# First FFN begun on x*(1+scale) with the shift as a bias vector, and the depthwise convolution as 16 channels by 8 phases

## The reference, cut

```python
mod = (silu(c) @ w_ada + b_ada)              # 9 D: sh1 sc1 gt1 sh2 sc2 gt2 sh3 sc3 gt3, scale as 1 + sc
h = x * (1 + sc1) + sh1
gt, up = split(h @ ffn1_w_in)                # hidden width 2816
x = layer_norm(ALPHA * x + 0.5 * gt1 * ((silu(gt) * up) @ ffn1_w_out))
h = x * (1 + sc2) + sh2
a, b, u, gate_a, gate_b = split(h @ w_in)    # 1024 columns each
glu  = a * sigmoid(b)
conv = causal_depthwise_conv(glu, width 31) + conv_b
y_a  = silu(layer_norm(conv)) @ w_conv_out
pooled = trailing_mean(u, window 2, 4, 8 or 16 by channel group) - u
y_b  = (group_matmul(pooled, pool_w) * pool_scale) @ w_pool_out
x = layer_norm(ALPHA * x + gt2 * ((sigmoid(gate_a) * y_a + sigmoid(gate_b) * y_b) @ w_out))
# then a second half-step FFN like the first, with sh3 sc3 gt3
```

## Time and profile before

| | |
|---|---|
| median of 3 runs | 1577.0 us (1576.28 to 1577.05) |
| the profiled execution | 1571.3 us; span on its slowest core 1569.7 us |
| spans of the 8 cores | 1556.7 to 1569.7 us, granted TensorE clock 0.992 to 0.995 |
| busy on the slowest core | PE 1479.4, PEld 856.3, DVE 688.6, ACT 472.9, POOL 133.9 us |
| DMA engines | mean 145 GB/s moved; the weight queue's packets took 48.6%, SP's 20.9% of 16 engines' span |
| chain that ended last | PE 84%, DMA 9%, DVE 3%, ACT 2%, issue 2% |

### The profile page before, as it was taken

How to read it: one execution, slowest core, us unless ns; L and a number is a source line. 1 busy time by engine, 2 the same in 40 slices (tenths; PEclk the granted TensorE clock), 3 DMA queues, 4 the chain that set the end, 5 groups by cost and what they waited for, 6 DMA issues and landing times.

```text
span 1569.7 us, 24460 instructions; the slowest of 8 cores (1556.7 to 1569.7 us)
## 1 busy us (share of the span) xinstructions
PE 1479.4 (94%) x9258; PEld 856.3 (55%) x9258; DVE 688.6 (44%) x935; ACT 472.9 (30%) x688; POOL 133.9 (9%) x253
## 2 busy tenths in 40 slices
PE   0799999999899999999999999999999999999995
PEld 0466666544344457765664564445666665444454
DVE  1223323565222465972377687237431134441255
ACT  0011112253112264672127456113531111421124
POOL 2011111000110000000000000000000010000000
PEclk9999999999999999999999999999999999999998
DMA  9989999869977868635386964457586465584522
GB/s 185 180 141 196 196 215 186 167 110 190 186 137 145 144 155 232 182 72 131 55 174 143 243 182 105 97 104 154 118 178 131 74 132 97 111 170 84 113 70 99
DMA packets 94980, 227.03 MB, mean 145 GB/s; under 512 B 10848, under 2 KB 36192, under 8 KB 94688
## 3 DMA queue, kind: packets, MB, share of 16 engines
q0 software_dynamic: 37136, 124.11, 48.6%
q1 hardware_dynamic: 57728, 101.36, 20.9%
HBM read 299.64 MB, written 40.11 MB: 216 GB/s over the span
## 4 chain that ended last, share of the span: by engine, by line
PE 84%; DMA 9%; DVE 3%; ACT 2%; issue 2%; SPq 0%; DVEq 0%; ACTq 0%; POOL 0%; POOLq 0%
PE ps L354 78%; PE ps L769 4%; DMA VS<-pool_w 3%; DMA ring<-ffn_w_in 2%; DMA VS<-R 2%; DMA XS<-tp_dr 1%; DMA ring<-w_ada 1%; DVE VB L322 1%; PE ps L418 1%; DVE hA L319 1%; ACT L315 1%; ACT scr L315 0%; PE ps L544 0%; ACT rstd_sb L315 0%; ACT VB L315 0%
## 5 line engine op out<-in xcount | busy, mean ns | idle before, releaser
L354 PE MATMUL ps<-hA,ring 128*128 128x348 bf16 x3072 | 467.2, 312 | 8.1 <-DMA ring<-ffn_w_in 3.6
L354 PE MATMUL ps<-hB,ring 128*128 128x512 bf16 x2048 | 450.9, 380 | 10.0 <-DVE mpv L513 5.3
L354 PE MATMUL ps<-R,ring 128*128 128x348 bf16 (+3 forms) x2378 | 398.7, 327 | 0.0
L354 PEld LDWEIGHTS ps<-hA,ring 128*128 128x128 bf16 x3072 | 298.1, 97 | 170.1 <-issue 9.6
L354 PEld LDWEIGHTS ps<-hB,ring 128*128 128x128 bf16 x2048 | 200.0, 98 | 250.6 <-issue 15.7
L315 ACT ACTIVATE scr<-ps 128x1044 f32<-128x1044 f32 (+1 forms) x136 | 140.3, 1032 | 633.8 <-PE ps L354 629.8
L354 PEld LDWEIGHTS ps<-R,ring 128*128 128x128 bf16 x2378 | 229.3, 97 | 163.1 <-issue 0.2
L319 DVE TENSOR_TENSOR R<-ps,scr 128x1024 bf16<-128x1024 f32 (+2 forms) x112 | 128.8, 1156 | 429.9 <-PE ps L354 387.0
L315 ACT ACTIVATE scr<-VB 128x1044 f32<-128x1044 f32 (+3 forms) x56 | 51.5, 919 | 296.8 <-DVE VB L322 121.1
L322 DVE SCALAR_TENSOR_TENSOR VB<-ps,modT,XS 128x1024 f32<-128x1024 f32 (+4 forms) x56 | 55.1, 983 | 97.1 <-PE ps L354 94.1
L303 POOL DMA_DIRECT2D ring<-ffn_w_in x88 | 46.6, 531 | 470.8 <-PE ps L354 440.2
(11 more groups left out here) (121 smaller groups left out, 802.7 us busy)
## 6 DMA issues: line engine op xcount, KB each, us to landing
ring<-ffn_w_in POOLq DMA_DIRECT2D x88, 512.0 KB, 10.0
ring<-w_in POOLq DMA_DIRECT2D x40, 512.0 KB, 7.5
ring<-w_ada POOLq DMA_DIRECT2D x36, 512.0 KB, 15.8
ring<-ffn_w_out POOLq DMA_DIRECT2D x48, 352.0 KB, 6.3
XS<-tp_dr SPq DMA_DIRECT2D x48, 288.0 KB, 4.5
tp_dr<-VS SPq DMA_DIRECT2D x32, 288.0 KB, 15.5
XS<-x_b SPq DMA_DIRECT2D x16, 512.0 KB, 9.8
VS<-R SPq DMA_DIRECT2D x128, 64.0 KB, 5.6
```

The lines of the kernel that those rows point to most:

```text
L354: ins = e.matmul(o, lt, rt[:, c0:c0 + n], start=(i == 0), stop=(i == nk - 1))
```

## The change

*The start.* The columns of `w_ada` keep their natural order: blocks 0 and 1 are the shift, 2 and 3 the scale of the first FFN. x of A is loaded in three DMAs, by column tile over all chunks. Blocks 2 and 3 come first; `hpre` = x * (1 + scale) is made tile by tile, on DVE and, each third chunk, on ACT. `ffn_in_early` runs FFN blocks 0 and 1 on it (block 0 in groups of one tile), keeping the raw products in f32. Then ada blocks 0 and 1, constants, and `shift_bias`: 64 matmuls of 17 columns of the same two weight blocks with the shift, whose result is the bias of the eight products. `h_shifted` makes the full h, and `ffn_in` runs from block 2. `finish_early` completes j = 0 to 3 with the biases in the hooks of j = 4 to 7.

*The adaLN blocks.* Two before the first FFN's matmuls, two after its block 1, 4 to 8 in `ffn_in` of A (j = 6, 9, ..., 18), 9 to 11 in `ffn_out` of A, none in `ffn_in` of B, 12 to 15 in the last gated stage of mixer A (oc = 1, 3, 5, 7), 16 and 17 in that of B (oc = 1, 5).

*The convolution.* NQ = 8 phases of 128 columns: 64 groups of 16 channels by 8 phases, ND = 5 matrices each, NTOEP = 12 buffers of five matrices. A conv unit has four groups, 20 matmuls of 128 columns; ACT does four Identities of 128 columns and one Square of 512 columns that reads the Identities' result; each group's matmuls wait for its own matrices alone. Moves and stores between the layouts are 8 DMAs per chunk, of 128 rows of 256 B each. The pooling works on 8 phases, with one more instruction for windows 8 and 16. `cwv` holds 5 x 8 columns for 64 groups and shares memory with hB; `build_toep` makes two groups at a time.

```diff
-NQ = 4
-NM = 256
-NG = 32
-ND = 9
-GHAL = 8
-UH = 6
+NQ = 8
+NM = 128
+NG = 64
+ND = 5
+GHAL = 4
+UH = 4
 UR = UH + NM
-NTOEP = 7
+NTOEP = 12
+TW = ND * 128
...
-            for i in range(4):
-                o = VB[:, 2 * i * GA.W:(2 * i + 2) * GA.W].rearrange("p (c n) -> p c n", c=2)
-                dma("sp", "s_x%d" % i, [(o, x_d["a"][2 * i:2 * i + 2].rearrange("c p n -> p c n"))], [], [o])
+            for i, (c0, n) in enumerate(GA.tiles):
+                o = XV[:, :, c0:c0 + n]
+                dma("sp", "s_x%d" % i, [(o, x_d["a"][:, :, c0:c0 + n].rearrange("c p n -> p c n"))], [],
+                    [chunk(VB, GA, c)[:, c0:c0 + n] for c in range(KC)])
...
-            for i in range(4):
-                ada_block(i)
-                for c in (2 * i, 2 * i + 1):
-                    h_main(GA, c, chunk(VB, GA, c), 0, "dve")
-                    h_samp(GA, c, chunk(VB, GA, c), 0)
+            mset(hpre[:, :, NP + SW:GA.W], 0.0)
+            ada_block(2)
+            ada_block(3)
+            for c0, n in GA.tiles:
+                n = min(n, NP - c0)
+                for c in range(KC):
+                    o, i_ = hp(c)[:, c0:c0 + n], chunk(VB, GA, c)[:, c0:c0 + n]
+                    if c % 3 == 2:
+                        act(o, i_, AF.Identity, scale=modp(1, c))
+                    else:
+                        S.add("dve", lambda e, o=o, i_=i_, s=modp(1, c): e.tensor_scalar_mul(out=o, in0=i_, scalar1=s),
+                              reads=[i_, modp(1, c)], writes=[o])
+            xs_ = XV[:, :, NP:NP + SW]
+            tt(hpre[:, :, NP:NP + SW], xs_, modT[:, 8:16, 1:17], ALU.mult)
...
+        def ffn_in_early(blk):
+            s = wblock(ffn_in_w[0][blk])
+            v = sl(s, KC, 512)
+            for jj in range(2):
+                j = 2 * blk + jj
+                groups = [[t] for t in range(GA.nt)] if blk == 0 else [list(range(GA.nt))]
+                for ts_ in groups:
+                    for b in range(2):
+                        o = b * 256 + jj * 128
+                        bk = bank(b, GA)
+                        mm([bk[t] for t in ts_], lambda k, o=o: v[:, k, o:o + 128], hp, KC)
+                act(P3(pre[2 * j], GA), pb(0, GA), AF.Copy)
+                cpy(P3(pre[2 * j + 1], GA), pb(1, GA))
+            return v
+
+        def shift_bias(vs):
+            cpy(shb, modT[:, 0:8, :])
+            for j in range(4):
+                for b in range(2):
+                    i = 2 * j + b
+                    o = b * 256 + (j % 2) * 128
+                    out = ps[:, 6, i * 17:(i + 1) * 17]
+                    mm([(out, 0, 17)], lambda k, o=o, j=j: vs[j // 2][:, k, o:o + 128], lambda k: shb[:, k, :], KC)
+            p6 = ps[:, 6, 0:136].rearrange("p (i t) -> p i t", t=17)
+            cpy(csb[:, :, :], p6[:, :, 1:17])
+            cpy(mpv[:, :, 0:1], p6[:, :, 0:1])
+
+        def h_shifted():
+            for c in range(KC):
+                h_main(GA, c, chunk(VB, GA, c), 0, "act" if c % 3 == 2 else "dve")
+            t = ctx[:, :, :]
+            tt(t, XV[:, :, NP:NP + SW], modT[:, 8:16, 1:17], ALU.mult)
+            tt(h_t["a"][:, :, NP:NP + SW], t, modT[:, 0:8, 1:17], ALU.add)
...
-                pairs = [(GP[:, 4 * c + i, GHAL:], st[32 * i:32 * i + 32, :].rearrange("c (q m) -> c q m", q=NQ)) for i in range(4)]
-                dma("sp", "gr%d" % (c % 2), pairs, [st], [GP[:, 4 * c:4 * c + 4, GHAL:]])
+                n = 128 // NQ
+                pairs = [(GP[:, NQ * c + i, GHAL:], st[n * i:n * i + n, :].rearrange("c (q m) -> c q m", q=NQ)) for i in range(NQ)]
+                dma("sp", "gr%d" % (c % 2), pairs, [st], [GP[:, NQ * c:NQ * c + NQ, GHAL:]])
 
             def tload(gi):
                 if gi < NG:
                     o = toep[gi % NTOEP]
-                    dma("sp", "tl%d" % (gi % NTOEP), [(o, tp_dr[gi])], [dk("tp_dr", gi)], [o])
+                    dma("sp", "tl%d" % (gi % NTOEP), [(o, tp_dr[gi // 2][:, (gi % 2) * TW:(gi % 2 + 1) * TW])], [dk("tp_dr", gi // 2)], [o])
...
+                for t in range(UG):
+                    gi = UG * u + t
+
+                    def cmm(e, gi=gi, t=t):
+                        ins = None
                         for d in range(ND):
                             ins = e.matmul(ps[:, bk, t * NM:(t + 1) * NM], toep[gi % NTOEP][:, d * 128:(d + 1) * 128],
                                            GP[:, gi, GHAL - d:GHAL - d + NM], start=(d == 0), stop=(d == ND - 1))
-                    return ins
-                S.add("pe", cmm, reads=[toep[(2 * u + t) % NTOEP] for t in range(2)] + [GP[:, 2 * u:2 * u + 2, :]],
-                      writes=[ps[:, bk, :]])
-                tload(2 * u + NTOEP)
-                tload(2 * u + NTOEP + 1)
+                        return ins
+                    S.add("pe", cmm, reads=[toep[gi % NTOEP], GP[:, gi, :]], writes=[ps[:, bk, :]])
+                for t in range(UG):
+                    tload(UG * u + t + NTOEP)
                 sq = sqc[u % 4]
-                for t in range(2):
-                    gi = 2 * u + t
+                for t in range(UG):
+                    gi = UG * u + t
                     act(conv[:, gi, :], ps[:, bk, t * NM:(t + 1) * NM], AF.Identity, bias=cpv[:, 0, gi:gi + 1])
-                    act(sq[:, t * NM:(t + 1) * NM], ps[:, bk, t * NM:(t + 1) * NM], AF.Square, bias=cpv[:, 0, gi:gi + 1])
+                cu = lambda w: conv[:, UG * w:UG * w + UG, :].rearrange("p t n -> p (t n)")
+                act(sq, cu(u), AF.Square)
...
-                            dma("sp", "sw%d" % (c % 4), [(d_[32 * i:32 * i + 32, :].rearrange("c (q m) -> c q m", q=NQ), s_[:, i, :]) for i in range(4)], [s_], [d_])
+                            dma("sp", "sw%d" % (c % 4), [(d_[nch * i:nch * i + nch, :].rearrange("c (q m) -> c q m", q=NQ), s_[:, i, :])
+                                                         for i in range(NQ)], [s_], [d_])
...
+                            if oc % 2 and oc in late_ada:
+                                ada_block(late_ada[oc])
...
-            if j == 1:
-                consts_early()
-            if j >= 2 and j % 2 == 0 and j <= 12:
-                ada_block(4 + (j - 2) // 2)
-            if j in (15, 19):
-                ada_block(10 + (j - 15) // 4)
+            if j < 8:
+                finish_early(j - 4)
+            if j in (6, 9, 12, 15, 18):
+                ada_block(4 + (j - 6) // 3)
             if j >= 6:
                 build_toep(2 * (j - 6))
                 build_toep(2 * (j - 6) + 1)
             if j == 20:
                 consts_late()
 
-        ffn_in(GA, 0, hook_f1in_a)
+        v0 = ffn_in_early(0)
+        v1 = ffn_in_early(1)
+        ada_block(0)
+        ada_block(1)
+        consts_early()
+        shift_bias([v0, v1])
+        h_shifted()
+        ffn_in(GA, 0, hook_f1in_a, 2)
         h0b = gen_h0b()
 
         def hook_f1out_a(oc):
             next(h0b, None)
             if oc == 0:
                 next(h0b, None)
-            if oc in (1, 4):
-                ada_block(12 + oc // 4)
+            if oc in (1, 3, 5):
+                ada_block(9 + oc // 2)
...
-            if j in (4, 9, 14, 19):
-                ada_block(14 + (j - 4) // 5)
...
-        mixer(GA, "xr1a", xr_d["a", 1])
+        mixer(GA, "xr1a", xr_d["a", 1], {1: 12, 3: 13, 5: 14, 7: 15})
         bg.add(gen_ln(GA, "ln2_g", "ln2_b", 6, xr_d["a", 2], "xr2a"))
-        mixer(GB, "xr1b", xr_d["b", 1])
+        mixer(GB, "xr1b", xr_d["b", 1], {1: 16, 5: 17})
...
```

193 lines of the change are left out of this document (106 added, 87 removed).

## The result

The changed kernel took 1648.5 us (median of four runs, 1646.6 to 1649.0) where the kernel before, run beside it, took 1577.0: a ratio of 1.045 (95% interval 1.043 to 1.046), some 71.5 us slower. The direction was the forecast's, the size was not: 10.5 us were forecast, and the range ended at 1603. The profiled execution took 1646.6 us. In some executions of every kernel the cores of one die, or of both, ran at a lower granted clock and took longer; all numbers here are of the other executions.

The account below looks back on a forecast made before the run. TensorE was taken as the bound, busy 1479.4 of 1569.7 us. Terms +21 - 6.5 + 4.5 - 17 + 6 + 2.5 = +10.5 us took the 1577.0 us median to 1587.5, range 1569 to 1603.

Parts of the forecast that it names:

- The start: Up to FFN block 2: x's last tile lands late and block 2 waits for its ring slot, +21 us.
- tiles 0 and 1 give TensorE only 32 matmuls: At the start: before x's last tile lands, TensorE can run 32 matmuls of block 0, under 5 us.
- adaLN out of the first FFN of B: pool_w lands earlier, so TensorE's wait for mpv and its low clock go: -6.5 us (0 to -7.3).
- Late adaLN in mixer A: Last gated stage: adaLN blocks take two ring slots, so weights come late: +4.5 us (+1 to +8).
- less at `w_out`: Mixer A: TensorE loses about 4 us at the gated stage's half turn, and less than that at w_out.
- The convolution's stretch: Both mixers: shorter matmuls save 27 us on TensorE, of which VectorE's bound leaves -17 us (-10 to -28).
- what is late next: Convolution: VectorE's unchanged sums become the limit, so conv_stats comes 9 us earlier in A and 8 in B.
- Rival (c): Convolution: 128-column matmuls are bound by loading weights, up to 0.08 us each, about 1592.5 us; 7 in 100.
- GLU moves: GLU stages: 8 smaller DMAs per chunk instead of 4 take SP longer and delay TensorE, +6 us (+2 to +14).
- Silus and ACT: Gated stages: twice as many silus at about 0.4 us put ACT's 7.3 us against TensorE's: +2.5 us (0 to +6).
- if SP falls behind: Stated sign, whole kernel: SP falling behind was one of three things that would show the prediction wrong.
- Rival (d): Mixers: SP and ACT become bounds, moves queue, silus wait for buffers: 1607 us, half of it 1599; 15 in 100.

Follow-up runs that it names:

- e4: Changed kernel with the sample columns' product split by chunk and the first ring slot's shift bias computed ahead of FFN block 1: 1633.5 us.
- e8: As e4, but x loaded as before, in four DMAs of two chunks with rows of 4176 B: 1621.6 us.
- e3: Changed kernel with the sample columns' product made by chunk, in eight instructions instead of one: 1640.9 us.
- e11: Kernel before, with pool_w loaded ahead of the sample pool state and one adaLN block moved from step 9 to 12: ratio 0.9989 to the kernel before.
- e1: Kernel before with only the change's start and adaLN order, convolution as before: 1617.0 and 1625.0 us beside 1573.7.
- e7: Changed kernel with adaLN blocks 12 to 15 back in the first FFN of group B: 1630.6 us.
- e2: Changed kernel with start and adaLN order undone, so the convolution's change alone: ratio 1.0157 to the kernel before.
- e10: Convolution change alone, with only every second Toeplitz matrix loaded and its neighbour reusing it: ratio 1.0046 to the kernel before.
- e9: Convolution change alone, with only four of the eight silu stores of each chunk: ratio 1.0055 to the kernel before.
- e13: Convolution change alone, with half the silu stores left out and only every second Toeplitz matrix loaded: ratio 0.995 to the kernel before.
- e14: Convolution change alone, with three of each chunk's eight silu stores issued from Pool's queue instead of SP's: ratio 1.0153 to the kernel before.
- e6: Changed kernel with Toeplitz matrices loaded in pairs, rows of 2560 B, ten buffers for twelve: 1645.0 us.

## Why the prediction was wrong

**The start, forecast +21, measured +30.5.** The landing of x's first tile, the turns by packets (e4 and e8), the wait for the ring slot (forecast 6, measured 7.2) and the slow matmuls behind it were right. The step that failed is "tiles 0 and 1 give TensorE only 32 matmuls": they gave one. I read which columns the sample product writes and not the range of bytes that it covers, which spans seven chunks of h; e3 shows that cost as 5.3 us. The waiting of Pool's queue I costed rightly and then took as fixed; e4 shows that an order without it was at hand. The rest is small: blocks 0 and 1 end 2 us later than forecast in e3 and the 64 matmuls with the shift 3 us later, as x's last tile came 2 us late, and behind the wait 144 matmuls take 24.2 us for 21.5, 2.7 lost where I had 2.0.

**adaLN out of the first FFN of B, forecast -6.5, measured -7.7 on the slowest core** (-10.9 less the 3.2 us of the blocks' own matmuls, which only change place), and -2.3 in the mean of the eight. The mechanism was right: without the blocks `pool_w` lands 14.0 to 17.1 us after its issue on every core, for 19.5 to 40.6, and no core waits. The size agrees by luck of the core: on five of the eight there was no stall to remove, so the slowest core of another execution can gain nothing, as e11 did.

**Late adaLN in mixer A, forecast +4.5, measured +13 to +15** (in the mean of the cores 13.8 for e1 against before and 12.7 for the changed kernel against e7; on the slowest core 15 in the last gated stage and `w_out`; each less the blocks' own 3.2). The mis-sized term is "less at `w_out`". The waits for weights were 7.1 us, near the forecast's reach. What I left out is the share of the DMA engines: with the late weights in it the stage around `w_out` runs at 1.02 of 16 engines, and the residual's loads, which never were in my list, take 7 us longer each. The lower clock behind the waits adds 2.6 us (3.56 and 2.94 us for 12 matmuls that take 1.94 at full clock).

**Late adaLN in mixer B, forecast nearly nothing, measured +2 to +4.** Its gated stages take 138.6 us in e1 for 132.9 before, and 147.5 in the changed kernel for 143.5 in e2, in the mean of the cores; 1.6 us of each are the two blocks' own. On the slowest cores alone it would be 4.9 and 8.8.

**The convolution's stretch, forecast -17, measured -2.5** (-5.9 in the mean of the cores). Three steps held: 0.056 us a matmul, VectorE's work unchanged (52.98 us busy in 61 before, 52.41 after), and VectorE as the bound, 18.3 us less in e10. The step that failed is "what is late next". I checked VectorE and asked of the Toeplitz loads only in B. These loads were late in A before the change as well, by 2.15 us: they were a third limit that lay almost level with TensorE's. By the time TensorE is quicker, they are what it waits for. Rival (c) is out with the first of them. The Trainium skill (TensorE: Matmul & The Clock Gate, Back-to-back issue gap) gives about 81 ns for a matmul of 128 columns in a stream of weight loads and matmuls; this trace has 56, and the measurement decides.

**GLU moves, forecast +6, measured +10** (3.8 and 6.2), within its ends. With the convolution alone the two stretches are 4.9 to 9.6 us longer than before in the mean of the cores (e2, e9, e10, e13, e14), so the size was right to low. Not all of the 10 is the moves': e1, which has the old ones, is 2.5 us longer there in the mean.

**Silus and ACT, forecast +2.5, measured about +20** (gated stages of e2 against before: 151.7 - 141.4 and 143.2 - 132.9 us; 9.9 and 10.6 in the mean of the cores). This is the largest error. I had named the moves and the stores together under "smaller DMAs", and then placed SP's load only in the GLU stage, against a chunk of 7.1 us. In the gated stage I costed ACT's silus (0.39 us each, for the 0.4 forecast) and left SP's 64 stores out: 47.8 us, where before the 32 took 24.9, and TensorE waits for what stands behind the silus on ACT. My own sign, "if SP falls behind", is what came. Rival (d), "silus wait for their four buffers, tanh for the silus", named the mechanism, and its ends for this stage, +6 and +8, come to two thirds of it; I gave it 15 in 100. (Its "half of it 1599" is a slip: half way from the forecast to its 1607 is 1597.)

**The sum.** 30.5 - 10.9 + 30.7 + 16.8 + 3.8 + 6.2 - 2.8 + 0.3 + 0.7 = 75.3 us, where the forecast had 10.5. Of the 64.8 us missed on the slowest core, 21 lie in the first gated stages (SP's stores of silu; 17.5 by e2), 14.5 in the convolution stretches (the Toeplitz loads), 9.5 in the start, 10.5 and 4 in the stages with the late adaLN blocks in A and B, 4 in GLU; FFN B gave 1.2 more than forecast, and 2 us remain. The means of the cores add up to 72.5 us. The medians lie 71.5 apart and not 75.3, since the profiled execution of the kernel before lay 5.7 us under its median and that of the changed kernel 1.9. What stays open is what makes the Toeplitz loads late. e10 shows only that half of them is in time, and e6 that issues and row size are not most of it. The nearest to a test is e14: its Pool queue stands at the stores and issues no weights in the convolution stretch of either mixer, where e2 issues two halves of `w_in` and two of the folded weights in each, and with all Toeplitz loads in place no wait for `tp_dr` is left at the end of the stretch in either mixer. As in e10, `conv_stats` then waits for VectorE. TensorE, e14:

```profile
676.40 0.60 PE L927 MATMUL ps<-R,bones_sb 128*128 128x256 bf16 x4 [3.90 <-DVE ghalo L331]
```

The two stretches take 57.3 and 56.8 us in the mean of the cores, for 60.4 and 61.5 in e2 and 55.8 and 53.2 in e10. So the turns with the weights would be 7.8 us of the 12.9 that e10 gains; no kernel that only moves these weights was run.

## What to carry to other kernels

For every stage, list the load of every queue and engine before and after the change, the issuing engine included: a store of 128 short rows took SP 0.75 us to issue here, and 64 of them set a stage's length. An engine that is made faster meets the next limit at once; look for it in waits that are small today, for a wait of 2 us can mean that a second limit lies level with the first. And begin early only what is complete: a matmul started on a third of the input gains nothing when its dependency covers the whole tile, and splitting the input's rows in three made its last part land 17 us later (65.2 us in e4, 48.4 in e8). Last, look at all cores before pricing a wait: one that three of eight cores meet is worth little where the next core is as late without it.

## What the runs showed of the hardware

- Two DMA queues shared the engines by packets: the same bytes of x in rows of 1392 B instead of 4176 B, beside weight rows of 4096 B, moved 230 packets to the weights' 233 (167 to 170 in long rows) and put the first matmul of FFN block 2 at 96.2 instead of 85.3 us (e4 and e8).
- SP's issue took 0.75 us in the mean for each store of 128 rows of 256 B (64 in 47.78) and 0.78 for each of 512 B before (32 in 24.94, of which 1.2 waiting); the median store took 0.583 and 0.590 us. With the same rows and half of the bytes it was the same.
- One load of the same program landed at very different times on the eight cores of one execution: `pool_w` after 19.5 to 40.6 us in the kernel before, beside adaLN weights, and after 11.3 to 15.1 in e11, issued ahead of the pool state and with one adaLN block moved behind it.
- Waits of TensorE of 7 to 14 us cost 1.4 to 2.7 us more in the matmuls behind them (5.09 for 3.72 in e7, 6.17 for 3.72, 24.2 for 21.5); behind the longest the granted clock was 0.65, between the levels 1.2 and 2.4 GHz. Behind a wait of 2.25 us that followed 32 matmuls of 17 columns, 12 matmuls took 3.56 for 1.94.
- Three of eight stores moved to the queue that also issues weights changed no bytes and yet held the weights up: in e14 they gave TensorE 19 us and took 23.6.
